# The first downward product of a hybrid block in the seven-product scheme, with its weight sums made by DMA

## The reference

```
ada = silu(c) @ w_ada + b_ada                     # 9 x 1024: shift, scale, gate of three sublayers
h = rmsnorm(x, g_ffn1) * (1 + scale0) + shift0
x = x + 0.5 * gate0 * ((silu(h @ Wgate) * (h @ Wup)) @ w_ffn1_down)      # hidden width 2816
h = rmsnorm(x, g_mix) * (1 + scale1) + shift1
x = x + gate1 * (mixer(h) @ w_out)                # 8 stick-breaking heads, 8 forgetting-attention heads
h = rmsnorm(x, g_ffn2) * (1 + scale2) + shift2
x = x + 0.5 * gate2 * (swiglu(h, w_ffn2_up) @ w_ffn2_down)
out = rmsnorm(x, g_final)
```

## Time and profile before

| what | us |
|---|---|
| median of 3 runs (lowest, highest) | 1070.68 (1070.48, 1071.17) |
| the profiled execution, its own time | 1069.39 |
| its span, first to last instruction | 1067.6 |
| PE busy in the span | 1051.3 (98%) |
| PE weight loads busy | 918.2 (86%) |
| DVE busy | 718.0 (67%) |
| ACT busy | 533.2 (50%) |
| POOL busy | 57.0 (5%) |

### The profile page before, as it was taken

The page is one execution under the profiler, slowest core; times in us unless marked ns, Lnnn a source line. Parts: engine busy times, 40 slices in busy tenths (PEclk is TensorE's granted clock), DMA queues, the critical chain, the costliest instruction groups (busy, mean ns, idle before and its releaser), DMA issues.

```text
span 1067.6 us, 17029 instructions
## 1 busy us (share of the span) xinstructions
PE 1051.3 (98%) x6432; PEld 918.2 (86%) x6432; DVE 718.0 (67%) x1064; ACT 533.2 (50%) x871; POOL 57.0 (5%) x92
## 2 busy tenths in 40 slices
PE   8999999999999999999999999999999999999997
PEld 5788888888888889889878877889999999999997
DVE  5745555555554547886876676579876676689873
ACT  6422322322322225775787577448645545566653
POOL 1000000000000001211111011000000000000000
PEclk9999999999999999999999999999999999999999
DMA  9878888896598784798699867425999799967652
GB/s 341 254 228 284 265 274 291 273 305 183 154 307 222 197 257 116 137 218 211 155 198 191 185 168 156 140 80 139 236 236 227 226 259 229 211 171 204 190 163 80
DMA packets 250433, 223.08 MB, mean 209 GB/s; under 512 B 6924, under 2 KB 222588, under 8 KB 248316
## 3 DMA queue, kind: packets, MB, share of 16 engines
q1 hardware_dynamic: 233776, 154.45, 50.6%
q0 software_dynamic: 16128, 67.11, 25.7%
q10 hardware_dynamic: 460, 0.58, 0.2%
HBM read 217.93 MB, written 67.11 MB: 267 GB/s over the span
## 4 chain that ended last, share of the span: by engine, by line
PE 90%; ACT 3%; SPq 3%; DVE 2%; issue 1%; DMA 1%; ACTq 0%; DVEq 0%
PE bank L982 28%; PE bank L984 28%; PE bank L983 28%; SPq L858 2%; PE bank L1348 1%; PE bank L1320 1%; DMA w_raw<-in_w_ffn_up_dram 1%; PE bank L1296 1%; PE bank L1297 1%; PE bank L1025 1%; ACT w_hi L1539 0%; ACT tmp_b L1929 0%; DVE pt_lo L2677 0%; PE bank L1490 0%; PE bank L1298 0%
## 5 line engine op out<-in xcount | busy, mean ns | idle before, releaser
L982 PE MATMUL bank<-h_hi,w_hi 128*128 128x512 f32 (+1 forms) x592 | 230.5, 389 | 0.0
L984 PE MATMUL bank<-h_hi,w_lo 128*128 128x512 f32 (+1 forms) x592 | 223.5, 378 | 0.0
L983 PE MATMUL bank<-h_lo,w_hi 128*128 128x512 f32 (+1 forms) x592 | 223.5, 377 | 0.0
L2085 DVE TENSOR_TENSOR w_lo<-w_raw,w_hi 128x1024 fp32r<-128x1024 f32 x97 | 118.7, 1225 | 152.7 <-ACT w_hi L1539 152.1
L1539 ACT ACTIVATE w_hi<-w_raw 128x1024 fp32r<-128x1024 f32 x97 | 102.5, 1057 | 200.9 <-PE bank L984 191.5
L982 PEld LDWEIGHTS bank<-h_hi,w_hi 128*128 128x128 f32 x592 | 111.8, 189 | 24.5 <-issue 2.6
L983 PEld LDWEIGHTS bank<-h_lo,w_hi 128*128 128x128 f32 x592 | 111.7, 189 | 24.3 <-issue 3.1
L984 PEld LDWEIGHTS bank<-h_hi,w_lo 128*128 128x128 f32 x592 | 111.6, 189 | 22.6
L2245 DVE TENSOR_TENSOR up_lo<-up_raw,up_hi 128x1024 fp32r<-128x1024 f32 x80 | 86.6, 1086 | 21.0 <-ACT up_hi L1638 21.0
L984 PE MATMUL bank<-combo,up_lo 128*128 128x256 f32 x320 | 90.6, 283 | 0.0
L982 PE MATMUL bank<-combo,up_hi 128*128 128x256 f32 x320 | 90.5, 283 | 0.0
(11 more groups left out here) (293 smaller groups left out, 2267.4 us busy)
## 6 DMA issues: line engine op xcount, KB each, us to landing
w_sums<-in_w_ffn_up_dram POOLq DMA_DIRECT2D x24, 1280.0 KB, 8.6
ada_w<-in_w_ada_dram SPq DMA_DIRECT2D x56, 512.0 KB, 4.4
w_raw<-in_w_ffn_up_dram SPq DMA_DIRECT2D x48, 512.0 KB, 6.9
up_raw<-w_sums SPq DMA_DIRECT2D x40, 512.0 KB, 6.0
d_sums<-in_w_ffn_down_dram POOLq DMA_DIRECT2D x12, 1408.0 KB, 9.2
w_raw<-in_w_in_dram SPq DMA_DIRECT2D x28, 512.0 KB, 5.8
d_raw<-d_sums SPq DMA_DIRECT2D x16, 704.0 KB, 4.7
w_sums<-w_sums POOLq DMA_DIRECT2D x8, 1280.0 KB, 10.4
```

The costliest lines, as they stand in the source:

```text
L982: mm(dst, wh, xh, start=start, stop=False, skip_group_check=skip)
L983: mm(dst, wh, xl, start=False, stop=False, skip_group_check=skip)
L984: return mm(dst, wl, xh, start=False, stop=stop, skip_group_check=skip)
L2085: v.tensor_tensor(w_lo[:, s, :], w_raw[:, r, :], w_hi[:, s, :].bitcast(F32), ALU.subtract)\
```

## The change

**First downward stage.** It takes the seven-product scheme of the second one: `down_chunk`, `down_high`, `down_low`, `moving_*`, `keep_out`, `add_out` and `last_update` get an argument e (0 first, 1 second), own banks, own places in memory, seven raw tiles and four high ones instead of six and five. The hidden block is kept in float32 (`hid1`), without high and low parts. P1's and P5's moving parts are split in the last steps of the upward stage. The squares for the norm are taken per quarter of x on ACT and folded on DVE (`fold_quarter`), the last quarter per chunk (`square_last`, `fold_last`), the first mixer tiles' low parts stand between the normed parts.

**Modulation products.** All 56 are made in the first upward stage, in shares per step `ADA_SHARES`, with a turn on PE behind the step in which a block's eighth is made. The loops over steps are written out. SP loads the tiles of step f, then the share of step f - 1; the first downward tiles follow the last share.

**Weight sums.** `d_sums` exists twice. In the first upward stage POOL issues 12 pieces for the first downward sums (copies and adding ones in pairs) and 4 upward copies; in the first downward stage the last 4 downward pieces and 2 upward copies; in the mixer the other 26 upward pieces; then 3 pieces of the second downward sums, and the other 13 in the second upward stage. The first mixer tiles are loaded behind chunks 24 and 25 of the downward stage.

The diff, cut to its core:

```diff
-DOWN_PARTS = ((0, 8), (8, 8), (16, 6))
-D_RAW, D_HI = 6, 5
+D_RAW, D_HI = (7, 6), (4, 5)
-UP_BLOCKS = (FC - 2) // 4
-DOWN_CHUNKS = (3, 3, 2, 0)
+ADA_SHARES = (4, 4) + (3, 3, 2) * 6
 T_DOWN1 = T_UP1 + 2 * FC
-T_MIX = T_DOWN1 + 3 * KC
+T_MIX = T_DOWN1 + N_DOWN
...
@@ gpsimd
+            for n, piece in enumerate(DOWN_PIECES[:12]):
+                copied_after(T_UP1 + 4 + 13 * n // 5)
+                down_piece(0, *piece)
+            for n in range(4):
+                copied_after(T_UP1 + 34 + 2 * n)
+                up_pieces(1)
+            for n, piece in enumerate(DOWN_PIECES[12:]):
+                copied_after(T_DOWN1 + 1 + 3 * n)
+                down_piece(0, *piece)
+            for n in range(2):
+                copied_after(T_DOWN1 + 13 + 6 * n)
+                up_pieces(1)
...
+            up_pieces(2)
             for j in range(1, JOBS):
                 repeat_k(j)
+                up_pieces((3, 4, 3, 2, 5, 2, 5)[j - 1])
+            for n, piece in enumerate(DOWN_PIECES):
+                if n >= 3:
+                    copied_after(uses(SEVEN0 + 1 + 4 * (n - 3) // 3, 3))
+                down_piece(1, *piece)
@@ sync
+            for f in range(2, FC):
+                load_up(0, T_UP1, f, f % 2)
+                if f > 2:
+                    load_share(f - 1)
+            load_share(FC - 1)
...
+            for t in range(N_DOWN):
+                load_down(0, t)
+            def load_mix(t, dst, src):
+                if t < T_MIX + RAW:
+                    sp.wait_ge(w_used, T_DOWN1 + 25 + (t - T_MIX) // 2)
+                load_w(t, t % RAW, dst, src)
...
-                    sp.wait_ge(sums_made, 16 * (N_PIECES + N_BEFORE))
+                    sp.wait_ge(sums_made, 16 * (N_PIECES + 16))
@@ tensor
-            with pe.Fori(0, UP_BLOCKS) as i:
-                for q in range(4):
-                    up_pair(T_UP1, 4 * i + 2 + q, q % 2, 0)
-                ada_turn(KC * i + 3 * KC, i + 4)
+            for f in range(2, FC):
+                up_pair(T_UP1, f, f % 2, 0)
+                if sum(ADA_SHARES[:f - 1]) % KC == 0:
+                    m = turned_blocks[0]
+                    ada_turn((m + 3) * KC, m + 4)
+                    turned_blocks[0] += 1
...
+            for i in (P1, P5, P2, P6, P7, P4, P3):
+                for n in range(4):
+                    down_chunk(0, i, n)
+                    if (i, n) == (P3, 1):
+                        side_sum(1, 0, 2)
...
-                if k == 3:
-                    side_sum(1, 1, 2)
+                if k == 2:
+                    side_sum(1, 1, 4)
@@ scalar
+            f = FC - 1
+            down_high(0, 0)
+            moving_high(0, P5, 2)
+            act.wait_ge(w_used, 2 * f + 1)
+            a(tmp_a[:, f % 2, :], bank[f % 2][:], ACT.Silu).then_inc(silu_done, 1)
+            down_high(0, 1)
@@ vector
+            for f in range(2, FC):
+                share = ADA_SHARES[f - 2]
+                for half in range(2):
+                    one_product()
+                    if f < FC - 1:
+                        split_lo(T_UP1 + 2 * f + half + SPLIT, half, (2 * (f % 2) + half + SPLIT) % RAW)
+                    elif half == 0:
+                        down_low(0, 0)
+                for _ in range(share - 2):
+                    one_product()
...
+                elif f == FC - 2:
+                    for j in range(3):
+                        moving_sum(0, P5, j)
+                elif f == FC - 1:
...
+                    moving_low(0, P5, 0)
+                    moving_low(0, P5, 1)
+                    down_low(0, 1)
+                hidden_first(f)
+                if products[0] % KC == 0:
+                    ada_sum(B_LOOP + blocks_made[0], 5 + blocks_made[0])
+                    blocks_made[0] += 1
...
+            last_update(0, 0)
+            last_update(0, 1)
...
+            fold_last(0)
+            fold_last(1)
+            low_apart(0, w6_hi, w6_lo)
+            side_normed(1, 0, 3)
+            side_low(1, 0, 2)
+            last_update(0, 2)
+            side_low(1, 0, 3)
+            side_normed(1, 0, 4)
+            last_update(0, 3)
+            low_apart(1, w7_hi, w7_lo)
+            fold_last(2)
+            fold_last(3)
```

More of the change, by code:

```diff
@@ L647, in product_bank @@
[L647 to L663, removed]
-            last = n if (i, n) in ((P3, 2), (P3, 3)) else n | 1
-            return T_DOWN2 + 4 * i + last + 1
+        t_down = (T_DOWN1, T_DOWN2)
@@ new lines, in evacuated, with added, last_added, chunk_done @@
+        def evacuated(e, s, n):
+            return KEPT * e + 4 * s + n + (s > 2 or s == 2 and n > 3)
+        def added(e, s):
+            return (X_DOWN1, X_DOWN2)[e] + sum(len(parts) for _, parts, _ in SETS[:s]) + (s > 2)
+        def last_added(e, n):
+            return added(e, len(SETS)) + n
+        def chunk_done(e, i, n):
+            last = n if (i, n) in ((P3, 2), (P3, 3)) else n | 1
+            return t_down[e] + 4 * i + last + 1
+        def down_landed(e, t):
+            slot = t % D_RAW[e]
+            return 16 * (t // D_RAW[e] + 1) + (0 if slot in (4, 5) else 16) + 64 * e
@@ L1755, in _ @@
[L1755 to L1761 removed]
+            for f in range(2, FC - 1):
+                up_chunk(f)
+                if 16 <= f < 19:
+                    moving_high(0, P1, f - 16)
+                elif f == FC - 2:
+                    moving_high(0, P5, 0)
+                    moving_high(0, P5, 1)
@@ new lines, in square_last @@
+            def square_last(n):
+                act.wait_ge(x_upd, last_added(0, n + 1))
+                act.wait_ge(sq_folded, 1)
+                a(sq_late[:, n, :], xT[:, n, side(1)], ACT.Square).then_inc(sq_done, 1)
+            act.wait_ge(gacc_done, 2)
+            for i in (P1, P5, P2, P6, P7, P4, P3):
+                for n in range(4):
+                    if P1 < i < P3:
+                        for j in HIGH_STEPS[n]:
+                            moving_high(0, i + 1, j)
+                    if n % 2 == 0 and (i or n):
+                        done = i if n else i - 1
+                        for m in range(2):
+                            for part, entry in enumerate(SETS):
+                                if entry[0] == done:
+                                    keep_out(0, part, 2 - n + m)
+                    if 4 * i + n + LEAD < N_DOWN:
+                        down_high(0, 4 * i + n + LEAD)
+                    if (i, n) in SQUARED:
+                        where = SQUARED[i, n]
+                        square_quarter(where, added(0, {"x11": 4, "x22": 6, "x21": 7}[where]))
```

696 lines of the change are left out of this document (333 added, 363 removed).

## The result

The changed kernel takes **1099.17 us** (median of 4 runs, 1096.96 to 1100.53) beside 1070.58 for the kernel before (4 runs): ratio 1.0267, 95% interval 1.0245 to 1.0288. It is slower by 28.6 us, where 0.8 was forecast, and outside the range of 1063 to 1081. The profiled execution has a span of 1098.7 us for 1067.6, 31.1 more.

The account below looks back on a forecast made before the run. PE was taken as the bound, never waiting, so matmul time and added waits count in full. 14.6 us gained against 15.4 lost made it 0.8 us slower: 1071.5 us, range 1063 to 1081.

Parts of the forecast that it names:

- The other five inner turns: First upward stage, turns after the first: two or three wait 0.5 to 2 us; loss 2 us, between 0 and 6.
- The clock: Behind the first turn's wait in the first upward stage: PE at half speed for a while; loss 1.5 us, 0 to 3.
- The first turn: First upward stage, near 80 us: PE waits for products behind a split and late loads; loss 6.2 us, 4.9 to 8.
- Matmuls: First downward stage: 924 matmuls of 256 columns replace 528 of 512, 124.7 us becomes 110.1; gain 14.6 us.
- The last turn: End of the first upward stage: the last product stands behind DVE's first low part; loss 2.7 us, 2 to 4.
- the border: First downward stage to mixer: DVE's late updates and low parts delay the second column sum; loss 2 us, 0.5 to 3.
- The third chunk's wait: Start of the first downward stage: chunk 2's low part at 23.9 where PE wants 23.1; loss 1 us, 0 to 2.
- Moved at no cost: Mixer: POOL's 26 transfers instead of 22 end near 707, before the first load of sums at 721.47; no loss.
- Second upward stage: Second upward stage: 13 transfers, 3 more directly ahead, where 6 ran before; loss 0, between 0 and 5 us.
- DMA becomes the bound: Rival, upward stages: loads beside accumulating transfers make splits wait; 1079 in its middle, 1085 at the far end; chance 0.22.
- late key copies: Mixer: key copies or sums coming late were listed among the signs that the forecast was wrong; no size given.

Follow-up runs that it names:

- g2_three: The changed kernel with three ada_w load buffers in place of two, order as in the changed kernel; 1074.02 us, ratio to before 1.0027.
- e3_four: The changed kernel with four ada_w load buffers in place of two, order and bytes kept; 1073.02 us, ratio to before 1.0015.
- f2_keys: f1_four_order with POOL's piece counts between the mixer's key copies set to 3, 4, 3, 2, 4, 2, 6; 1062.83 us, ratio to before 0.9929.
- g1_two_order: The changed kernel, two buffers kept, with products moved ahead on DVE only in steps with a share of four and the last step; 1096.89 us.
- e1_light: The changed kernel with the first upward stage's 12 first-downward-sum pieces moving 4 rows each in place of 704, sums not made; 1073.83 us.
- f1_four_order: e3_four plus g1_two_order's order of products on DVE; 1064.45 us, ratio to before 0.995.
- e4_late: The changed kernel with the second upward stage's 13 pieces at 4 rows each and one mixer piece moved behind the seventh key copy; 1096.41 us.
- f3_spread: f2_keys with second-downward-sum pieces spread: nine in the second upward stage, every second step, four in the second downward stage; 1060.37 us, ratio 0.990.

## Why the prediction was wrong

**The other five inner turns: the step that failed.** "Two or three of the five turns should wait 0.5 to 2 us. Loss 2 us, between 0 and 6." All five waited: 5.03, 0.68, 3.98, 1.57 and 3.31, 14.6 us. The formula was right (a pair costs landing + 1.28 + 0.5), its input was not. I had taken the landing of the kernel before (4.4 us) everywhere but in the accumulating pairs, and let the chain catch up between them. The median landing became 6.3, and (6.3 + 1.8) / 2 = 4.05 us a product against 4.2 wanted leaves almost no slack, so a late load stayed on the path. The 4.4 was the median of all 56 loads of the kernel before, of which 40 ran in the first upward stage beside 14 copies and no adding piece (4.2 us); here 56 run in that stage beside 16 pieces, six of them adding. By the same formula three buffers at 7.2 us give 3.0 and four at 7.6 give 2.35, and g2_three and e3_four wait nothing there.

**The clock.** "Loss 1.5 us, between 0 and 3", for the first turn: 2.6 there, in range. But it was counted for one turn, where four turns of the stage were followed by half speed: 9.0 us in all, and 1.7 more behind the last turn, in the downward stage. This second part of the error follows from the first: the wait of 3.98 us cost 6.8. The Trainium skill ("TensorE: Matmul & The Clock Gate", Part 1) says that idleness throttles the array. The turns of the changed kernel agree: 0.50 behind each wait of 3.3 us and more, full speed behind 0.7 and 1.6. But the length of a wait alone does not tell what follows it: 2.97 us in the mixer, 2.14 in f2_keys and 1.79 in e3_four (at 628.37) were followed by 0.50, and 3.81 in g1_two_order was not. What else decides stays open.

**The first turn.** 6.2 (4.9 to 8) predicted, 7.94 measured. Both causes that the step named were real, the split and the two buffers; g1_two_order (6.46 us left) and e3_four (5.05) show that each alone holds most of the wait.

**Matmuls.** 110.1 us for the stage predicted, 112.09 measured, 1.7 of the difference the half-speed start; e1_light's stage takes 111.19 and f1_four_order's 111.17. Against 124.7 the gain is 12.6 in the changed kernel and 13.5 in those two, of 14.6 predicted: right but for a microsecond. It shows in the time once the turns no longer wait (f1_four_order, 6 us under the kernel before).

**The last turn and the border.** 2.7 us (2 to 4) predicted, 3.41 measured. The third chunk's wait of 1 us did not come. The border was put at 2 us (0.5 to 3) and cost 0.2, under its range: PE waited 0.85 us at the second column sum, and the rest of the stretch was about as much shorter than before.

**Moved at no cost: half right.** The last sums of POOL were issued at 721.46 and had landed when a downward piece followed at 732.01, well ahead of the second upward stage's column sum at 750.80: the cover held. What I had named only as a sign of error, late key copies, is where PE waited in the mixer, which lost 3.8 us: 2.97 and 0.66 us of wait, and some 3.2 us at half speed behind the first. I had asked when POOL ends, not what is in flight when a small urgent copy is issued.

**Second upward stage.** 0 (0 to 5) predicted, 3.0 measured; e4_late shows that the pieces make it, and f3_spread that fewer of them, further apart, do not.

**The rivals.** "DMA becomes the bound" had the place, the sign and a time 14 us too low at its far end. As a bound of bandwidth it is false (e3_four moves more bytes a second with no wait at six turns); as longer landings it is true (e1_light). It named splits as what would wait; the turns did. The bounds of the single terms were the fault of the range: 0 to 6 for five turns at the landing of the kernel before, and a clock term that did not scale with the number of waits.

**The error in one sum.** The spans differ by 31.1 us where 0.8 was forecast, 30.3 too little. In it are the inner turns with 12.6, the clock in the upward stage with 7.5, the mixer with 3.8, the second upward stage with 3.0, the matmuls with 2.0, the first turn with 1.7, the tails with 1.3, the last turn with 0.7 and the split with 0.5; the border and the third chunk, put too high, take 2.8 off.

## What to carry to other kernels

A stream of loads that each wait for the use of their own buffer takes (landing + use) / buffers per load. When a change asks for more loads in the same time, work that out with the landing that the new traffic will give, and ask how many buffers it takes for the slack to survive a landing twice as long; one buffer more was worth some 25 us here, with the same bytes. Where a wait has two sufficient causes, undoing either shows little: try both together before either is dismissed. Behind a wait PE may work at half speed for a while, which cost 1.7 to 2.8 us each time at the turns here. Count that for every wait of 3 us and more, and not once for the kernel; shorter waits can bring it too.

## What the runs showed of the hardware that was not expected

A 512 KB load issued beside an adding piece took up to 14.2 us (10.5 to 14.2 in 110 to 127), where 3.5 is the shortest in the kernel. In e3_four a mean share of 0.98 and 294 GB/s stood together with no wait of PE at six of seven turns: a full share is no proof that DMA is the bound. The seventh key copies, of 128 KB, took 6.5 to 7.1 us beside an adding piece of their own queue, and 4.1 before, without one. But this varies: others beside an adding piece took 4.0 to 5.1 us (issued at 574.3 in the changed kernel) and 7.7 to 9.2 (at 549.9 in the kernel before). At the last turn the clock fell only behind the wait: PE was idle from about 320.0 to 323.4, the transposes still ran at full pace, and half speed held from about 324.6 to 328.0. The longest wait without a fall behind it was 3.81 us (g1_two_order). In f3_spread the clock was at 0.50 in 44 to 46 though no wait of PE of 0.2 us or more stands in 30 to 50:

```profile
44.00:46.00 2.00, 2.00 (x6) 1.54 (x6) 1.90 (x5) 2.00 (x3) 0.00 (x0) 0.50 1.16 292
```
